# Inverting unit triangles in blocks of 32 rather than 64 for the first four levels

## What is computed

```python
a_mat = jnp.where(strict, jnp.einsum('bnhid,bnhjd->bnhij', k_beta, k) * decay, 0.0)
t_mat = a_mat + jnp.eye(CHUNK, dtype=jnp.float32)
solve = lambda rhs: lax.linalg.triangular_solve(t_mat, rhs, left_side=True, lower=True, unit_diagonal=True)
value = solve(v * beta[..., None])
k_cum = solve(k_beta * jnp.exp(gc)[..., None])
```

## Time and profile before

| | us |
|---|---|
| median of 3 runs | 3484.59 (3483.98 to 3485.78) |
| the profiled execution | 3487.36 |
| its span, first to last instruction | 3485.6 |
| PE busy | 3373.1 (97%) |
| DVE, ACT, POOL busy | 2252.5 (65%), 1620.8 (46%), 56.6 (2%) |
| mean granted clock of PE | 0.986 |

### The profile page before, as it was taken

The page is one execution under the profiler, slowest core; times in us unless marked ns, Lnnn a source line. Parts: engine busy times, 40 slices in busy tenths (PEclk is TensorE's granted clock), DMA queues, the critical chain, the costliest instruction groups (busy, mean ns, idle before and its releaser), DMA issues.

```text
span 3485.6 us, 68747 instructions
## 1 busy us (share of the span) xinstructions
PE 3373.1 (97%) x30086; PEld 3319.7 (95%) x30086; DVE 2252.5 (65%) x3653; ACT 1620.8 (46%) x2339; POOL 56.6 (2%) x78
## 2 busy tenths in 40 slices
PE   7999999999998999999999999998999999999997
PEld 7999999999998888899999999998998999999997
DVE  5656655556676688696666655687546976666455
ACT  5544444444455534364444444464443644444443
POOL 0000000000000000000000000001000000000000
PEclk9999999999999999999999999999999999999998
DMA  6455555555564322255555666542543465555663
GB/s 230 163 176 176 174 176 185 175 180 176 176 197 134 106 89 86 94 171 197 194 194 194 195 191 191 188 151 82 166 147 127 158 199 194 194 194 191 194 198 127
DMA packets 162494, 586.38 MB, mean 168 GB/s; under 512 B 18128, under 2 KB 18128, under 8 KB 161936
## 3 DMA queue, kind: packets, MB, share of 16 engines
q1 hardware_dynamic: 160560, 574.01, 50.4%
q0 software_dynamic: 1632, 7.96, 0.8%
HBM read 579.80 MB, written 2.10 MB: 167 GB/s over the span
## 4 chain that ended last, share of the span: by engine, by line
PE 53%; DVE 8%; ACT 1%; issue 0%; POOL 0%; ACTq 0%; DVEq 0%; POOLq 0%
PE bank L2082 16%; PE bank L2084 16%; PE bank L2083 16%; DVE pairs L2871 2%; PE bank L2295 1%; PE bank L2282 1%; DVE xs L2987 1%; DVE xs L2985 0%; PE bank L2097 0%; PE bank L2099 0%; PE bank L2098 0%; ACT pairs L2548 0%; DVE xr L2955 0%; DVE xr L2875 0%; DVE xs L2901 0%
## 5 line engine op out<-in xcount | busy, mean ns | idle before, releaser
L2082 PE MATMUL bank<-xr,pairs 128*128 128x256 f32 (+1 forms) x5888 | 1660.9, 282 | 35.2 <-DVE pairs L2871 27.3
L2083 PE MATMUL bank<-xr,pairs 128*128 128x256 f32 (+1 forms) x5888 | 1640.3, 279 | 0.0
L2084 PE MATMUL bank<-xr,pairs 128*128 128x256 f32 (+1 forms) x5888 | 1640.2, 279 | 0.0
L2548 ACT ACTIVATE pairs<-raw 128x1024 fp32r<-128x1024 f32 (+1 forms) x1106 | 1143.4, 1043 | 981.3 <-PE bank L2084 791.7
L2871 DVE TENSOR_TENSOR pairs<-raw,pairs 128x1024 fp32r<-128x1024 f32 (+1 forms) x1106 | 1306.3, 1200 | 383.2 <-ACT pairs L2548 380.1
L2082 PEld LDWEIGHTS bank<-xr,pairs 128*128 128x128 f32 x5888 | 1115.7, 189 | 45.9 <-DVE pairs L2871 30.1
L2083 PEld LDWEIGHTS bank<-xr,pairs 128*128 128x128 f32 x5888 | 1113.9, 189 | 1.3
L2084 PEld LDWEIGHTS bank<-xr,pairs 128*128 128x128 f32 x5888 | 1113.3, 189 | 0.0
L2082 PE MATMUL bank<-parts,pairs 128*128 128x256 f32 x1792 | 496.5, 277 | 0.4 <-DVE parts L2875 0.4
L2084 PE MATMUL bank<-parts,pairs 128*128 128x256 f32 x1792 | 495.0, 276 | 0.0
L2083 PE MATMUL bank<-parts,pairs 128*128 128x256 f32 x1792 | 495.0, 276 | 0.0
(11 more groups left out here) (601 smaller groups left out, 3069.3 us busy)
## 6 DMA issues: line engine op xcount, KB each, us to landing
raw<-in_w_in SPq DMA_DIRECT2D x176, 512.0 KB, 4.5
raw<-in_gate SPq DMA_DIRECT2D x176, 512.0 KB, 5.5
raw<-in_val SPq DMA_DIRECT2D x176, 512.0 KB, 4.4
raw<-in_down SPq DMA_DIRECT2D x160, 512.0 KB, 4.4
raw<-in_l_w_in SPq DMA_DIRECT2D x144, 512.0 KB, 4.0
raw<-in_w_out SPq DMA_DIRECT2D x64, 512.0 KB, 4.8
raw<-in_l_w_out SPq DMA_DIRECT2D x64, 512.0 KB, 3.9
raw<-in_v_in SPq DMA_DIRECT2D x48, 512.0 KB, 5.3
```

Source lines behind the costliest of these rows:

```text
L2082: mm(o, wh[:, q, :], rh[:, k, :], start=begin and q == 0, stop=False)
L2083: mm(o, wh[:, q, :], rl[:, k, :], start=False, stop=False)
L2084: last = mm(o, wl[:, q, :], rh[:, k, :], start=False, stop=end and q == c - 1)
L2548: e.activation(pair_of(n)[0], v3(raw_of(n), widths[n] // slices[n]), ACT.Copy).then_inc(*hi_made(n))
```

## The change

Levels 0 to 4 never mix the rows of different 32 x 32 diagonal blocks. The changed kernel holds, for these levels, only the diagonal blocks of 32: four on the partitions (`QUARTERS`), each with 32 columns, so tiles of 128 x 128 (4 triangles x 32 columns) in place of 128 x 256. Level 5 and 6 are as before. In j.proom lie Pq, Xq and Tq.

```diff
@@ invert
+    QUARTERS = [(slice(32 * k, 32 * k + 32), slice(32 * (k % 2), 32 * (k % 2) + 32)) for k in range(4)]
+        j.Pq, j.Xq, j.Tq = (v3(j.proom[:, i * 128:(i + 1) * 128], 4) for i in (0, 1, 3))
@@ PE inv_p
+            if n < 5:
+                p4 = v3(bk.view[:, 0:128], 4)
             for g in range(4):
-                if n < 6:
+                if n < 5:
+                    for b, c in QUARTERS:
+                        last = mm(p4[b, g, :], j.XT[b, g, 64 + c.start:64 + c.stop], j.Xq[b, g, :], start=True, stop=True)
+                elif n == 5:
                     for b, c in HALVES:
                         last = mm(p4[b, g, :], j.XT[b, g, 64:128], j.X[b, g, :], start=True, stop=True)
@@ PE inv_x
-            w.wait_ge(*vec["inv_XT", j.id, n - 1])
-            for g in range(4):
-                for b, _ in HALVES:
-                    if n < 5 or b.start == 0:
-                        last = mm(p4[b, g, :], j.T64[b, g, :], j.P1[b, g, :], start=True, stop=True)
+            w.wait_ge(*(vec["inv_XT", j.id, n - 1] if n > 1 else pool["inv_Tq", j.id]))
+            if n < 5:
+                p4 = v3(bk.view[:, 0:128], 4)
+                for g in range(4):
+                    for b, _ in QUARTERS:
+                        last = mm(p4[b, g, :], j.Tq[b, g, :], j.Pq[b, g, :], start=True, stop=True)
@@ ACT inv_add
-            if n < 5:
-                e.activation(j.X, p4, ACT.Copy).then_inc(*act("inv_X", j.id, n))
+            if n < 4:
+                e.activation(j.Xq, v3(bk.view[:, 0:128], 4), ACT.Copy).then_inc(*act("inv_X", j.id, n))
+            elif n == 4:
+                w.wait_ge(*pool["inv_Tq", j.id])
+                for b, c in QUARTERS:
+                    last = e.activation(j.X[b, :, c], v3(bk.view[:, 0:128], 4)[b], ACT.Copy)
+                last.then_inc(*act("inv_X", j.id, n))
@@ DVE inv_first
-            w.wait_ge(*pool["inv_I", j.id])
+            w.wait_ge(*pool["inv_Tq", j.id])
             w.on(j.inv_after)
-            e.tensor_tensor(j.T64, j.XT[:, :, 64:128], h4(C("lvl1t")), MUL).then_inc(*vec("inv_XT", j.id, 0))
-            w.wait_ge(*vec["inv_XT", j.id, 0])
-            e.transpose(j.X, j.T64).then_inc(*vec("inv_X", j.id, 0))
+            e.transpose(j.Xq, j.Tq).then_inc(*vec("inv_X", j.id, 0))
@@ DVE inv_mask, inv_add
+            if n < 5:
+                e.tensor_tensor(j.Pq, v3(bk.view[:, 0:128], 4), mask(n), MUL).then_inc(*vec("inv_mask", j.id, n))
+                if n < 4:
+                    e.transpose(j.Tq, j.Xq).then_inc(*vec("inv_XT", j.id, n))
+                else:
+                    e.transpose(j.T64, j.X).then_inc(*vec("inv_XT", j.id, n))
@@ POOL inv_start
             w.on(j.inv_after)
+            e.memset(j.room[:, 0:T], 0.0).then_inc(*pool("inv_room", j.id))
             e.memset(j.XT[:, :, 0:64], 0.0).then_inc(*pool("inv_zero", j.id))
...
             w.wait_ge(*pool["inv_I", j.id])
+            for b, c in QUARTERS:
+                last = e.tensor_tensor(j.Tq[b], j.XT[b, :, 64 + c.start:64 + c.stop], h4(C("lvl1q"))[b], MUL)
+            last.then_inc(*pool("inv_Tq", j.id))
+            w.wait_ge(*pool["inv_Tq", j.id])
```

More of the change, by code:

```diff
@@ L74 @@
     [("cos", 256), ("sin", 256), ("dlb", 512), ("nam", 64)],
-    [("bones", 128), ("rot64", 128), ("causal", 256), ("lvl", 6 * 64), ("lvl1t", 64), ("ident2", 64), ("gmask", 256), ("cap", 128)],
+    [("bones", 128), ("rot64", 128), ("causal", 256), ("lvl5", 64), ("lvlq", 4 * 32), ("lvl1q", 32), ("ident2", 64), ("gmask", 256), ("cap", 128)],
 ]
@@ L132, in constants @@
     lv = [np.logical_or(m, np.eye(64)) for m in lv]
-    put("lvl", np.tile(np.concatenate(lv, 1), (2, 1)))
-    put("lvl1t", np.tile(lv[0].T, (2, 1)))
+    put("lvl5", np.tile(lv[5], (2, 1)))
+    put("lvlq", np.tile(np.concatenate([m[0:32, 0:32] for m in lv[1:5]], 1), (4, 1)))
+    put("lvl1q", np.tile(lv[0][0:32, 0:32].T, (4, 1)))
     put("ident2", np.tile(np.eye(64), (2, 1)))
@@ L393, in h4 @@
     def h4(ap):
-        return ap.unsqueeze(1).broadcast_to([128, 4, 64])
+        return ap.unsqueeze(1).broadcast_to([128, 4, ap.shape[1]])
     def mask(n):
-        return h4(C("lvl", n * 64, n * 64 + 64))
+        return h4(C("lvl5") if n == 5 else C("lvlq", (n - 1) * 32, n * 32))
     x = v3(xs[:, :], KT)
@@ L2290, in inv_x @@
             w.wait_ge(*vec["inv_mask", j.id, n])
-            w.wait_ge(*vec["inv_XT", j.id, n - 1])
-            for g in range(4):
-                for b, _ in HALVES:
-                    if n < 5 or b.start == 0:
-                        last = mm(p4[b, g, :], j.T64[b, g, :], j.P1[b, g, :], start=True, stop=True)
-            if n == 5:
+            w.wait_ge(*(vec["inv_XT", j.id, n - 1] if n > 1 else pool["inv_Tq", j.id]))
[5 more added lines that the diff above has]
+            else:
+                for g in range(4):
+                    last = mm(p4[0:64, g, :], j.T64[0:64, g, :], j.P1[0:64, g, :], start=True, stop=True)
                 for g in range(4):
@@ L3227, in inv_first @@
         def inv_first(j):
-            w.wait_ge(*pool["inv_I", j.id])
+            w.wait_ge(*pool["inv_Tq", j.id])
             w.on(j.inv_after)
-            e.tensor_tensor(j.T64, j.XT[:, :, 64:128], h4(C("lvl1t")), MUL).then_inc(*vec("inv_XT", j.id, 0))
-            w.wait_ge(*vec["inv_XT", j.id, 0])
-            e.transpose(j.X, j.T64).then_inc(*vec("inv_X", j.id, 0))
+            e.transpose(j.Xq, j.Tq).then_inc(*vec("inv_X", j.id, 0))
         def inv_mask(j, n, bk):
             w.wait_ge(*pe["inv_p", j.id, n])
-            e.tensor_tensor(j.P1, v3(bk.view[:, 0:T], 4), mask(n), MUL).then_inc(*vec("inv_mask", j.id, n))
+            if n < 5:
+                e.tensor_tensor(j.Pq, v3(bk.view[:, 0:128], 4), mask(n), MUL).then_inc(*vec("inv_mask", j.id, n))
+            else:
+                e.tensor_tensor(j.P1, v3(bk.view[:, 0:T], 4), mask(n), MUL).then_inc(*vec("inv_mask", j.id, n))
         def inv_add(j, n, bk):
@@ L3240, in inv_add @@
                 w.wait_ge(*act["inv_X", j.id, n])
-                e.transpose(j.T64, j.X).then_inc(*vec("inv_XT", j.id, n))
+                if n < 4:
+                    e.transpose(j.Tq, j.Xq).then_inc(*vec("inv_XT", j.id, n))
+                else:
+                    e.transpose(j.T64, j.X).then_inc(*vec("inv_XT", j.id, n))
             else:
```

## The result

| | before | changed |
|---|---|---|
| median of the timed runs, side by side | 3484.73 us (3483.98 to 3485.78) | 3528.81 us (3525.94 to 3543.26) |
| ratio | | 1.0135, 95% interval 1.0107 to 1.0163 |
| profiled execution, its span | 3487.36, 3485.6 us | 3525.94, 3524.2 us |

I had predicted 3480.2 us, with 3488.5 as the upper end.

The account below looks back on a forecast made before the run. PE, busy in 97% of the span, was taken as the bound. Covered steps -5.0, delta-rule burst -1.8 and two RWKV bursts with the slow clock +2.4 gave -4.4 us, so 3480.2 us; range 3474 to 3488.5.

Parts of the forecast that it names:

- Step of PE: Levels 0 to 4 of the inversions: a step takes 0.26 us, shorter by 0.21 us; 96 steps change.
- covered RWKV steps: RWKV jobs 7 and 8, between weight products: each step's 0.21 us gained in full, part of 24 x 0.21 = 5.0 us.
- last delta-rule job: Its steps stand between weight products: 0.21 us gained on each, 1.7 us less in all.
- Rivals 2: PE steps: fixed load or issue cost holds a quarter's record at 58 ns; +4.5 us, 3489; chance 0.07.
- rival 3: PE steps: quarters run one after the other, a step takes 1.02 us; +50 us, 3535; chance 0.06.
- A round in a burst: One level of three jobs: 1.82 us instead of 2.89, bound by the chain over ACT and DVE.
- the sum of a burst: Each RWKV burst: head, round, single copies, later steps and tile switches add to -0.5 us, before any slow clock.
- The head: Start of each inversion job: POOL's extra memset and four products (1.45 us) make it net 1.25 us longer.
- The clock: RWKV bursts: a PE gap of 2.9 us probably drops the clock to 0.50 for 6.8 us, +1.7 us a burst.
- the likeliest case: Low clock in both RWKV bursts, making each +1.2 us instead of -0.5; chance 0.38.
- The delta-rule burst: Three delta-rule jobs, 2379 to 2417: earlier start and shorter rounds give -1.8 us, between 0 and -3.
- The rest of the kernel waits for nothing that the inversions hold: Stages outside the inversions: nothing there waits on them, so a lead of PE is kept.

Follow-up runs that it names:

- with pairs: Changed kernel, each 32 x 32 matmul of levels 1 to 4 taking the moving columns of two triangles, so 8 matmuls a step, not 16: 3499.7 us, ratio 1.0045.
- long head: Kernel before, with POOL's four products of 128 columns added ahead of the inversion's first product, which waits for them: 3498.4 us, ratio 1.0035.
- the short head: Changed kernel with one POOL product over all 128 partitions in place of the four, every PE instruction kept: 3518.5 us, ratio 1.0102.
- the gap of 160: Kernel before with an unused tensor of 160 columns behind the constants, moving vec and xs by 640 bytes a partition: 3503.0 us, ratio 1.0052.
- all causes taken away: Changed kernel with matmuls over two triangles, one POOL product in place of four, and vec and xs at their places of before: 3472.1 us, ratio 0.9966.
- the kernel with twice the instructions: Kernel before, each product of 64 moving columns in the first five levels written as two of 32: 3581.6 us, ratio 1.0279, two executions.

## Why the prediction was wrong, step by step

- **Step of PE: right.** I took 0.26 us. The sixteen covered RWKV steps saved 2.4 us where 16 x 0.21 = 3.4 was forecast (2.4 to 2.9 in the other kernels with the same steps), the eight of the last delta-rule job 1.5 where 1.7 was. With half the instructions it is 3.3 to 3.6 and 2.2, so the instructions' number costs something here too. Rivals 2 (the record doesn't shrink) and 3 (the quarters go singly) are refuted: the starts of a step spread over 0.26 us, and a step is 0.45 us from first start to last end. With rival 3 falls the rule that I cited from the Trainium skill, "TensorEngine Tiling (Array Packing)", Restrictions and Gotchas, on row tiles in one PSUM bank: the trace doesn't bear it out for quarters either.
- **A round in a burst, "1.82 us": this is the step that failed.** It was built from the chain over ACT and DVE with PE's steps in between, all fed at once. The prediction named it among the ways to be wrong ("if PE cannot be fed with twice the instructions in half the time") and gave it no chance and no price. A sign of it was in the trace of before: a step is 32 instructions (16 matmul records with their loads) in 0.467 us, 256 in 3.7, and the packets in the burst came 3.8 to 4.6 us apart. How near that was to a limit only the changed kernel shows. The change asked for 256 in 1.9 us at the lower clock and in 1.1 at the full one. Between the stops 256 took 3.47 to 4.01 us. What it costs is the difference of +36.2 in the changed kernel and +7.7 with pairs: 28 us. Taking the head alone away gives 20 in the traces (from 36.2 to 16.0) but only 10 by the medians, as the profiled execution was the fastest of its four. The long head added to the kernel before costs 10.5 in its trace. So the split is rough: the supply is the larger part, and the parts need not add, since a stop or a wait at the lower clock is paid with slower steps.
- **A sum that didn't use its own term.** The text gives a whole round 1.05 us and counts two of them; the sum of a burst takes 0.8 for one and 0.1 for the round with single copies. That is about 1 us a burst and explains nothing of the 36.
- The page "Runtime: NRT & Kernel Launch" of the Trainium skill, Instruction fetch mechanics, says that instructions are brought in blocks of 16 KiB, 256 of them, and that crossing a block is mostly hidden. Packet size and number agree with the trace; "mostly hidden" holds for the covered steps and not for the bursts, where seven crossings cost 1.3 to 2.1 us each.
- **The head: right in kind, too small.** Forecast +1.25 us, with 0.4 of it on the path for the second job, and a wait of 2.9 for the third; in burst 1 the second job's wait went from 0.99 to 2.52 us and the third's from 1.15 to 3.55. POOL's four products take 1.79 us and not 1.45, as the timeline of POOL has it for the third job:

```profile
1224.76 1.33 POOL L3580 TENSOR_TENSOR far<-right,con 64x256 f32<-64x256 f32 x2 [0.49 <-DVE right L3259]
1226.17 1.79 POOL L3584 TENSOR_TENSOR right<-far,con 32x128 f32<-32x128 f32 x4
```

- **The clock: direction right, length wrong.** It fell in both RWKV bursts, as the likeliest case had it, but stayed low for 17 and 44 us, not for 6.8. With pairs, behind the same wait of 3.56 us and without the stops, it was low for 3.4 us (7 us in burst 1 in all, for 20 in the changed kernel); with the short head and the stops, for 17. So in burst 1 the long stretch goes with the stops and not with the head; in burst 2 the short head took 44 us down to 14 with the stops in place, so there the head counts too. These are single traces, and what sets the clock down each time stays open.
- **The delta-rule burst: -1.8 forecast, +7.0 measured.** Two of the stops "issue" are in it, and the clock is low for 38 us. With pairs it is +2.1, with all causes taken away -1.0. The low clock by itself costs little there: with the instructions of before and the gap of 160 it is low for 20 us, at +0.9.
- **"The rest of the kernel waits for nothing that the inversions hold": the second step that failed.** The sentence is true of waits, but it put the change's effect on all other stages at nothing, and no wait carries the 16 us of the FFN. The change made the masks smaller, which moved xs. The diff shows it in the sizes of the constants, and I read these as a saving in columns only. As in before, the places of xr and pairs are set on purpose, by constants; that should have made me ask what else moves.
- The sum with the measured terms: covered and last job -3.9, bursts +36.2, FFN +15.9, the rest -9: +39 us in the span, as the two profiled executions have it. The medians are 5 us further apart, of which no trace was kept.

## What to carry to other kernels

Before you cut a small matmul into more and smaller ones, count PE's instructions (matmul records and weight loads) per microsecond where they run back to back: here the supply held at about 256 in 3.5 to 4 us, and a burst that was at 3.7 before had next to nothing left to give. Such a stop can be told by three signs: PE idle "issue" inside a group of matmuls, the same number of instructions from one to the next, and an end at a fixed distance behind an instruction packet. Where such steps lie between longer products the cut pays; in a burst, put more columns behind each weight load.

Whenever an edit changes the size of a tensor in SBUF, compare the rate of products in stages that it doesn't touch: keep the places first, then judge the edit.

## What the runs showed of the hardware that I had not expected

- Stops of PE of 1.3 to 2.1 us at every 256th instruction, when 256 are used up in less than about 3.5 us several times in a row, each ending 1.4 to 1.6 us after a packet of 16 KB has landed (1.2 to 1.5 with the short head). A shorter run above that rate passes (352 in 3.98 us, with pairs).
- A weight product of PE takes 113.2 or 117.6 ns, by where a tensor that PE doesn't read stands in SBUF: slow when it moved by -896 or +640 bytes, not when it moved by 0 or +256.
- In the kernel with twice the instructions the granted clock stood at 0.50 for some 71 us with PE busy in 70.89 of 71.00.
- An fp32 record costs 29 to 30 ns with 64 x 64 weights, with 32 or 64 moving columns alike, two such tiles running side by side. With 32 x 32 weights, four side by side, it costs 8 ns (32 records in 0.26 us).
